# Statistics of two rows on ScalarE, other orders at two norm boundaries, copies ahead of preparation, and last columns apart

## What is computed

```python
def first_block(x, c, ...):
    x = layer_norm(x, emb_ln_g, emb_ln_b)
    sh1, sc1, gt1, sh2, sc2, gt2 = split(silu(c) @ w_ada + b_ada, 6)
    p = (x * (1.0 + sc1) + sh1) @ w_in
    mix = concat([gmlp(p[..., :1024]), rwkv7(p[..., 1024:])]) @ w_out
    x = layer_norm(ALPHA * x + gt1 * mix, ln1_g, ln1_b)      # boundary 1
    gu = (x * (1.0 + sc2) + sh2) @ w_ffn_in                  # hidden size 2816
    f = (silu(gu[..., :2816]) * gu[..., 2816:]) @ w_ffn_out
    return layer_norm(ALPHA * x + gt2 * f, ln2_g, ln2_b)     # boundary 2

def second_block(x, ...):
    u = rms_norm(x, norm_mix_pre) @ w_in                     # behind boundary 2
    y = concat([sparse_attention(u), short_conv(u)]) @ w_out
    x = x + rms_norm(y, norm_mix_post)
    gu = causal_dwconv(rms_norm(x, norm_ffn_pre) @ w_ffn_up, ffn_conv_w)
    y = (gelu(g) * up) @ w_ffn_down                          # g, up: halves of gu
    return x + rms_norm(y, norm_ffn_post)
```

## Time and profile before

| | |
|---|---|
| Median of 3 runs | 1444.79 us (1439.49 to 1449.67) |
| Profiled execution | 1449.72 us |
| Its span, first to last instruction | 1447.9 us |
| Mean granted TensorE clock | 0.982 |
| Instructions | 23058 |
| HBM traffic | 146.5 MB |

### The profile page before, as it was taken

The page is one execution under the profiler, slowest core; times in us unless marked ns, Lnnn a source line. Parts: engine busy times, 40 slices in busy tenths (PEclk is TensorE's granted clock), DMA queues, the critical chain, the costliest instruction groups (busy, mean ns, idle before and its releaser), DMA issues.

```text
span 1447.9 us, 23058 instructions
## 1 busy us (share of the span) xinstructions
PE 1380.8 (95%) x9570; PEld 1140.0 (79%) x9570; DVE 697.5 (48%) x1197; ACT 562.3 (39%) x846; POOL 468.9 (32%) x132
## 2 busy tenths in 40 slices
PE   5999999899999999999998999999999999999998
PEld 3788766776888888888887678888788888888886
DVE  6645586463664433453336525687355445443002
ACT  4444554252343223222124434555355343343122
POOL 0223243024324434434520231112213344344344
PEclk9999999998999999999999989999999999999999
DMA  8763166002222232233213520101221322322311
GB/s 334 241 137 114 59 239 229 3 4 87 88 88 88 87 117 88 87 116 116 88 61 124 202 88 4 56 30 59 74 88 59 117 87 88 116 88 102 116 58 58
DMA packets 24741, 147.93 MB, mean 102 GB/s; under 512 B 2716, under 2 KB 3868, under 8 KB 9024
## 3 DMA queue, kind: packets, MB, share of 16 engines
q1 hardware_dynamic: 21128, 134.21, 25.4%
q10 hardware_dynamic: 3512, 12.26, 3.3%
HBM read 141.74 MB, written 4.72 MB: 101 GB/s over the span
## 4 chain that ended last, share of the span: by engine, by line
PE 84%; DVE 7%; ACT 3%; issue 2%; POOL 2%; DMA 2%; SPq 0%; DVEq 0%; ACTq 0%; POOLq 0%
PE bank L2073 23%; PE bank L2075 22%; PE bank L2074 22%; PE bank L2377 5%; PE bank L1169 2%; POOL weight_lo L1302 2%; DMA raw<-in_weights 2%; PE bank L1160 1%; PE bank L1151 1%; PE bank L2256 1%; ACT weight_hi L1350 1%; PE bank L2190 1%; PE bank L2237 1%; PE bank L1078 1%; DVE xres L1685 1%
## 5 line engine op out<-in xcount | busy, mean ns | idle before, releaser
L1302 POOL TENSOR_TENSOR weight_lo<-raw,weight_hi 128x2048 fp32r<-128x2048 f32 (+2 forms) x91 | 418.4, 4598 | 834.8 <-ACT weight_hi L1350 834.7
L2073 PE MATMUL bank<-act_hi,weight_hi 128*128 128x512 f32 (+1 forms) x1136 | 434.1, 382 | 10.0 <-POOL weight_lo L1302 3.7
L2075 PE MATMUL bank<-act_hi,weight_lo 128*128 128x512 f32 (+1 forms) x1136 | 424.6, 374 | 0.0
L2074 PE MATMUL bank<-act_lo,weight_hi 128*128 128x512 f32 (+1 forms) x1136 | 424.6, 374 | 0.0
L1350 ACT ACTIVATE weight_hi<-raw 128x2048 fp32r<-128x2048 f32 (+1 forms) x98 | 185.2, 1891 | 398.3 <-PE bank L2075 397.5
L2073 PEld LDWEIGHTS bank<-act_hi,weight_hi 128*128 128x128 f32 x1136 | 215.6, 190 | 52.1 <-issue 8.6
L2075 PEld LDWEIGHTS bank<-act_hi,weight_lo 128*128 128x128 f32 x1136 | 215.3, 190 | 38.5
L2074 PEld LDWEIGHTS bank<-act_lo,weight_hi 128*128 128x128 f32 x1136 | 215.6, 190 | 34.5
L2074 PE MATMUL bank<-weight_lo,hid_hi 128*128 128x512 f32 x352 | 136.9, 389 | 0.0
L2073 PE MATMUL bank<-weight_hi,hid_hi 128*128 128x512 f32 x352 | 136.9, 389 | 0.0
L2075 PE MATMUL bank<-weight_hi,hid_lo 128*128 128x512 f32 x352 | 136.9, 389 | 0.0
(11 more groups left out here) (370 smaller groups left out, 1760.1 us busy)
## 6 DMA issues: line engine op xcount, KB each, us to landing
raw<-in_weights SPq DMA_DIRECT2D x120, 1024.0 KB, 4.6
w<-in_w ACTq DMA_DIRECT2D x2, 2048.0 KB, 11.9
bias_rows<-grow ACTq DMA_DIRECT2D x1, 2560.0 KB
xres<-in_x SPq DMA_DIRECT2D x4, 512.0 KB, 6.2
strip<-bias_rows ACTq DMA_DIRECT2D x1, 2048.0 KB, 9.5
out<-xres SPq DMA_DIRECT2D x3, 512.0 KB, 2.6
row_a<-in_ln_g ACTq DMA_DIRECT2D x2, 512.0 KB, 4.1
row_b<-in_ln_b ACTq DMA_DIRECT2D x2, 512.0 KB, 4.9
```

Of the source, the lines that this page charges most:

```text
L1302: pool.tensor_tensor(wlo[i % SPLIT][:, :size], raw[n % RAW][:, :size], whi[i % SPLIT][:, :size], ALU.subtract).then_inc(lo_ready, 1)
L2073: pe.matmul(o, l[0], r[0], start=first, stop=False)
L2074: pe.matmul(o, l[0], r[1], start=False, stop=False)
L2075: return pe.matmul(o, l[1], r[0], start=False, stop=last)
```

## The change

- **Who makes low parts.** VectorE no longer makes that of slc, and makes those of up1_2 (behind boundary 1) and up2_2 (behind boundary 3); GpSimd makes slc's.
- **Input projection.** The steps of `ACT_EARLY` run in the next unit's turn of the loop, behind its `convert()` and ahead of its drains.
- **Boundary 1.** The turn of the first half stands ahead of the last tile's products of the last out1 unit. ScalarE normalises a half's first row as soon as its root is there, ahead of the copy of up1_0 in the first half, and ahead of the root of the second row. VectorE takes the reciprocal of the first row between the gating and the sums of the second row (first half), or ahead of them (second half).
- **Boundary 2.** Statistics of tiles 1 and 3 are taken by ScalarE (`rows_stats`: one pass with an accumulator for the mean, one of squared differences, the root); VectorE only writes the sum (`scaled_rows`), and its first normalising pass of tiles 1 and 3 reads `xres`, for tile 3 in place. So the banks of tile 3 are drained by `scaled_rows`, ahead of tile 2's normalisation. The copy of slc stands ahead of `affine_half`.
- **The end.** In `squares_of_rows` the first sum is scaled between the two squares. The last tile of the last ff2 unit is multiplied by column halves: both k of the first bank, then both of the second.

```diff
@@ -133,7 +133,7 @@
 RAW, SPLIT = 3, 2
-BY_VECTOR = [UNIT_AT[name] for name in ("lora0", "k0", "out1_3", f"down1_{FT // 2 - 1}", "slc", "out2_3", "up2_1")]
+BY_VECTOR = [UNIT_AT[name] for name in ("lora0", "k0", "out1_3", f"down1_{FT // 2 - 1}", "out2_3", "up2_1", "up1_2", "up2_2")]
@@ build
...
+    S = {n: sem(n) for n in ("summed", "gated", "row2_ready", ...
...
@@ -800,12 +800,12 @@
-            for j in range(2):
+            first, second = squares[:, 2 * t:2 * t + 1], squares[:, 2 * t + 1:2 * t + 2]
+            for j, total in enumerate((first, second)):
                 await_full(act, (stage, t, j))
-                a.step(act.activation(temp[:, 0:SEQ], bank((stage, t, j))[:], ACT.Square,
-                                      accum_out=squares[:, 2 * t + j:2 * t + j + 1]), drain((stage, t, j), "act"))
-            first, second = squares[:, 2 * t:2 * t + 1], squares[:, 2 * t + 1:2 * t + 2]
-            a.step(act.activation(first, first, ACT.Identity, bias=eps[:, 1:2], scale=1.0 / DM))
+                a.step(act.activation(temp[:, 0:SEQ], bank((stage, t, j))[:], ACT.Square, accum_out=total), drain((stage, t, j), "act"))
+                if j == 0:
+                    a.step(act.activation(first, first, ACT.Identity, bias=eps[:, 1:2], scale=1.0 / DM))
             a.done(act.activation(rstd[:, t:t + 1], second, ACT.Sqrt, bias=first, scale=1.0 / DM), S["rms_root"])
@@ -1045,8 +1045,7 @@
             affine_lo_half("h4", half, "nfp")
-            if half == 0:
-                low_part("up2_1")
+            low_part(f"up2_{1 + half}")
         for m in range(FT):
@@ -1450,9 +1449,11 @@
-        for name in W_IN1:
+        for name, previous in zip(W_IN1, ("", *W_IN1)):
             if name not in ("lora1", "k1", W_IN1[-1]):
                 convert()
+            for step in ACT_EARLY.get(previous, ()):
+                prep_act(*step)
             if name in ("lora0", "lora1"):
@@ -1469,15 +1470,11 @@
                     bias_rows()
-                for step in ACT_EARLY.get(name, ()):
-                    prep_act(*step)
             elif name[:2] == "pu":
...
                            drain((name, j), "act"))
-                for step in ACT_EARLY.get(name, ()):
-                    prep_act(*step)
                 if name == "pu1":
@@ -1610,10 +1605,10 @@
             root_of_variance(2 * half, TT + 2 * half)
+            normalise_row(2 * half)
             if half == 0:
...
             root_of_variance(2 * half + 1, TT + 2 * half + 1)
-            normalise_row(2 * half)
             normalise_row(2 * half + 1)
@@ -1638,12 +1633,24 @@
-            if (e, t) == (0, 2):
-                act.wait_ge(S["row2_ready"], 2)
+            if e == 0 and t >= 2:
+                act.wait_ge(S["row2_ready"], 2 * (t - 1))
             else:
...
+        def rows_stats(t):
+
+            if t == 1:
+                act.wait_ge(S["summed"], 2)
+            else:
+                for j in range(2):
+                    await_drained(act, ("ff1", t, j), "dve")
+            mean, var = mv[:, t, 0:1], mv[:, t, 1:2]
+            a.step(act.activation(xn2[:, t, :], xres[:, t, :], ACT.Identity, scale=1.0 / DM, accum_out=mean))
+            a.step(act.activation(xn2[:, t, :], xres[:, t, :], ACT.Square, bias=mean, scale=-1.0, accum_out=var))
+            a.done(act.activation(rstd[:, t:t + 1], var, ACT.Sqrt, bias=eps[:, 0:1], scale=1.0 / DM), S["root1"])
+
         def root_x(e, t):
@@ -1655,17 +1662,17 @@
             t, u = 2 * half, 2 * half + 1
-            root_of_variance(t, 2 * TT + t)
+            root_of_variance(t, 2 * TT + half)
+            rows_stats(u)
             if half == 0:
                 convert()
-            root_of_variance(u, 2 * TT + u)
             for x in (t, u):
...
                 scaled_x(0, x)
-            affine_half("h3", half, "nmp")
             if half == 0:
                 convert()
+            affine_half("h3", half, "nmp")
         second_act(act, a, convert, affine_half, square_x, root_x, scaled_x)
@@ -1956,13 +1963,15 @@
-        def residual(stage, t, gate, keep=False):
+        def residual(stage, t, gate, keep=False, between=()):
...
                     tt(bank((stage, t, j))[:], bank((stage, t, j))[:], gate[:, h], ALU.mult)
+            for x in between:
+                inverse(1 + x, x)
             for j, h in enumerate(halves):
@@ -1971,6 +1980,13 @@
             d.step(V.bn_aggr(mv[:, t, :], stats[:]), S["var1"])
+
+        def scaled_rows(t, sem=None):
+
+            for j in range(2):
+                name, h = ("ff1", t, j), slice(SEQ * j, SEQ * j + SEQ)
+                await_full(dve, name)
+                stt(xres[:, t, h], xres[:, t, h], ALPHA, bank(name)[:], ALU.mult, ALU.add, sem=sem or drain(name, "dve"))
@@ -2002,12 +2018,15 @@
                 residual("mix1", t, acc[:, 0:DM])
-            residual("mix1", u, acc[:, 0:DM])
-            for x in (t, u):
-                inverse(1 + x, x)
+            if half:
+                inverse(1 + t, t)
+            residual("mix1", u, acc[:, 0:DM], between=() if half else (t,))
+            inverse(1 + u, u)
             if half == 0:
...
             affine_lo_half("h2", half, 2)
+        low_part("up1_2")
+
         def gated_unit(n):
@@ -2035,10 +2054,10 @@
             halves = [slice(SEQ * j, SEQ * j + SEQ) for j in range(2)]
-            kept = t != 2
+            kept = t < 2
             of = [bank(("ff1", t, j))[:] if kept else xres[:, t, h] for j, h in enumerate(halves)]
             for j, h in enumerate(halves):
-                stt(of[j], of[j], mv[:, t, 0:1], row2_a[:, h], ALU.subtract, ALU.mult)
+                stt(of[j], of[j] if t == 0 else xres[:, t, h], mv[:, t, 0:1], row2_a[:, h], ALU.subtract, ALU.mult)
             for x in between:
@@ -2050,17 +2069,15 @@
             if half == 0:
-                residual("ff1", u, None, keep=True)
+                scaled_rows(u, S["summed"])
+            else:
+                scaled_rows(u)
             second_norm(t)
-            if half:
-                residual("ff1", u, None, keep=True)
             second_norm(u, between=(t,))
...
             affine_lo_half("h3", half, "nmp")
-            if half == 0:
-                low_part("slc")
         second_dve(dve, d, ts, tt, stt, affine_lo_half, inverse_x, low_part)
@@ -2122,10 +2139,10 @@
-        def rows_product(stage, n, n_units, weights, parts, t, k, turned=False):
+        def rows_product(stage, n, n_units, weights, parts, t, k, turned=False, banks_of=range(2)):
             (hi, lo), (hi_in, lo_in) = weights, parts
-            for j in range(2):
+            for j in banks_of:
                 c, f = slice(SEQ * j, SEQ * j + SEQ), 2 * ((n + 2) % 4 if turned else n) + k
@@ -2148,7 +2165,7 @@
                 if n == n_units - 1:
-                    order = [(t, k) for t in range(TT) for k in range(2)]
+                    order = [(t, k) for t in range(TT - 1) for k in range(2)]
                 if ready is not None and n in ready:
@@ -2159,6 +2176,9 @@
             if not halves:
+                for j in range(2):
+                    for k in range(2):
+                        rows_product(stage, n_units - 1, n_units, weights, parts, TT - 1, k, turned, (j,))
                 return
@@ -2195,7 +2215,7 @@
             for half in range(2):
-                if (half, stage) not in ((1, "h2"), (0, "h4")):
+                if (half, stage) not in ((1, "h2"), (0, "h2"), (0, "h4")):
                     turn_half(stage, half, source, ready)
@@ -2594,7 +2614,8 @@
-        dense_rows("mix1", "out1", 4, (act_hi, act_lo), begun, {2: (S["y_lo"], 2), 3: (S["y_lo_last"], 2)})
+        dense_rows("mix1", "out1", 4, (act_hi, act_lo), begun, {2: (S["y_lo"], 2), 3: (S["y_lo_last"], 2)},
+                   turn=("h2", xres, (S["xn_ready"], TT)))
         dense_halves(("up1_0", "up1_1"), "h2", xres, (S["xn_ready"], TT))
```

More of the change, by code:

```diff
@@ L603, in build @@
                                           "bias", "out", "rel", "tabs", "w1", "strip0", "strip", "rows3", "rows4")}
-    S = {n: sem(n) for n in ("gated", "row2_ready", "consts_ready", "silu_c", "future_ready", "xn_ready", "affine1", "h_hi", "h_lo", "shift_ready", "lora_ready",
+    S = {n: sem(n) for n in ("summed", "gated", "row2_ready", "consts_ready", "silu_c", "future_ready", "xn_ready", "affine1", "h_hi", "h_lo", "shift_ready", "lora_ready",
                              "kk_raw", "kk_sq", "cs_ready", "exp_ready", "minus_ready", "r_ready", "ep_ready", "rows_free", "root_ready", "inverse_ready", "norm_root", "prep_ready",
```

## The result

| | before | after |
|---|---|---|
| Median, runs of one occasion | 1444.23 us (1438.23 to 1451.87, 7 runs) | 1428.95 us (1428.15 to 1432.88, 7 runs) |
| Ratio | | 0.9883, 95% interval 0.9861 to 0.9906 |
| Profiled execution | 1449.72 us | 1430.69 us |
| Its span | 1447.9 us | 1428.9 us |
| Mean granted clock | 0.982 | 0.989 |

The account below looks back on a forecast made before the run. TensorE, busy 1380.8 of 1447.9 us, was taken to bound the kernel. Terms of 3.4 + 3.4 + 6.4 + 0.8 + 0.4 = 14.4 us off the median 1444.79 gave 1430.4 us, range 1422 to 1440.

Parts of the forecast that it names:

- Input projection: At v1, pv1 and pu0: TensorE's waits for GpSimd's low parts go, 3.4 us gained, bounds 0 and 3.5.
- Boundary 1: mix1 to up1: VectorE's and ScalarE's rows come sooner, up1_2's wait goes; 3.4 us gained, bounds 1.6 and 4.
- Boundary 2: ff1 to cmp, slc: less work on VectorE, shorter wait, last turn at full clock; 6.4 us gained, bounds 4.4 and 7.
- chain of collisions: Input projection: GpSimd's earlier low parts block VectorE near 103, 126 and 140 to 145; slack at pu1 at least 1.4 us.
- projection eaten: Rival at the input projection: collisions hold VectorE longer, pu1's low part becomes the new wait; gain 11, 1434 us; chance 0.15.
- Collision: Rival at boundary 2: tile 1's normalising pass overlaps GpSimd's cmp, TensorE starts 3.9 us later; gain 10.5, 1434.3 us; chance 0.12.
- up2_2 and the end: up2_2's low part on VectorE gains 0.8 us; at the end, earlier squares and scaling gain 0.4 us.
- bank claim: At up2_2: TensorE claims a bank drained after two operations of up2_0's convolution; 0.2 us given back.
- clock helps more: Rival: fewer waits spare half-clock stretches elsewhere, 2 to 8 us more; 1425 us; chance 0.11.
- within 1%: Whole kernel: change too small to tell from none, chance 0.56, against 0.40 faster and 0.04 slower; bound at 1430.3 us.

Follow-up runs that it names:

- e9: The changed kernel with the first turn of boundary 1 behind the last products again, all else as changed; one run, 1433.6 us.
- e3: The kernel before with only boundary 2 changed; 1434.53 us (4 runs), ratio 0.9910.
- e6: The changed kernel once more, unchanged, with a second profile; 1429.68 us (6 runs), ratio 0.9880.
- e11: The changed kernel with boundary 2 as before; 1437.18 us (6 runs), ratio 0.9935.
- e12: The kernel before with only boundary 2 changed, same kernel as e3 on another occasion; 1438.80 us (10 runs), ratio 0.9944.
- e7: The changed kernel with slc's low part back on VectorE; 1431.84 us (4 runs), ratio 0.9896.
- e10: The kernel before with 36 idle matmuls in TensorE's wait ahead of boundary 2's second turn; 1443.40 us (10 runs), ratio 0.9989.
- e8: The changed kernel with slc's high copy behind the activation copies, as before; 1427.97 us (4 runs), ratio 0.9872.
- e5: The kernel before once more, unchanged, with a second profile; 1447.68 us (12 runs), ratio 1.0000.

## Why the prediction was right

**Bound and method.** TensorE's starts decide; each term was read as "who ends last here". All five places came out within 0.4 us of their terms (boundary 2 in the first pair 6.8 for 6.4, the others 0.1), and the sum 0.5 above, 14.9 for 14.4 (14.6 with boundary 2's 6.4 of the other traces).

- **Input projection, forecast 3.4.** 3.5 measured, no wait at the three units. The chain of collisions went as forecast (103, 126, and 139 instead of 140 to 145), and pu1's low part came at 157.8, within 157.1 to 158.4. So "projection eaten" did not happen. One detail was missed: which operation the lock hits at 126.
- **Boundary 1, 3.4.** 3.5. With all borders moved by 3.55 us, the last turn starts 1.84 sooner (402.84 for 404.68, forecast 2.1). The last product of up1_1 starts 2.2 sooner (419.23 for 421.44), so some 0.4 goes with the clock of turn and products (forecast 0.3); 1.1 more is gained at up1_2 (forecast 0.99) and 0.1 behind it. e9 gives the early turn its 0.6; the two other changes of order weren't run apart.
- **Boundary 2, 6.4.** 6.4 in e3, e6, e11 and e12; 6.8 against the first trace, whose slow stretch was the longer. On the clock of before, moved by 7.02, VectorE's last row ends at 777.5 (forecast 777.9), the last diagonal at 779.7 (780.15), the wait is 0.55 (0.3). Half 0 gave 0.7 where 0.3 was forecast. Parts: slc 2.2 (e7; 2.29), clock 1.4 to 1.8 (e10; 1.9); the rest is put down to statistics and root, which no run took by themselves.
- **Collision.** Forecast at 755.0 to 756.6 against GpSimd's start at 757.0; measured 747.98 to 749.54 against 749.99, that is 755.00 to 756.56 against 757.01 on the clock of before. It missed by 0.45 us, where the forecast had 0.4. e8 shows what it would have cost.
- **up2_2 and the end, 0.8 and 0.4.** 0.86 and 0.32, with 0.23 left ahead of up2_2 (forecast 0.2). The profile names no releaser for it; VectorE's second convolution operation there ends at about 1084.3 (four from 1082.71 in 3.10 us), just ahead of TensorE's 1084.34, as the forecast's bank claim has it.
- **Clock elsewhere.** The profiled execution took 1430.69 us where 1435.3 was forecast, and 4.4 of this are in attention. Its stretch at half clock was 17.1 us in before and 6.8 in the changed kernel, but also 6.8 in the unchanged e5, and 17.1 again in the changed e7 and e9. Row of e7:

```profile
842.70:859.80 17.10, 16.19 (x55) 13.93 (x55) 7.51 (x27) 3.71 (x13) 3.46 (x1) 0.50 0.18 62
```

So this differs from execution to execution, with the change and without it. Whether the long stretch has become rarer isn't shown: it stands in five of the seven traces with the old boundary 2 and in two of the seven with the new.

**The 1%.** The chances leaned to "within 1%" (0.56), and the result is 1.2%, its interval 0.94% to 1.39%. What the sum lacked is gain beyond its five places: the medians of the first occasion are 15.3 us apart for the 14.4 of the sum. Over the 70 runs the mean of before is 1446.8, e6's is 1429.5: 17.3 us. The base doesn't explain this, since 14.4 off 1446.8 is 1.0% too. But it made the time look better than the sum was: 1444.79, the median of three runs of a kernel whose runs differ by 14 us, lay 2.0 under the long mean, and that hid most of the 2.9 that the gain lacked. That the time came out 1.5 us off is in this part luck.

The mark of the clock fell by 8.7 us (22.3 to 13.6). The stretches at half clock that went at the boundaries (3.4 to 6.8 between 387 and 408, 3.4 to 6.8 between 775 and 788, over the traces of kernels with the old order there) make 3.4 to 6.8 of it; what is left are fewer or shorter stretches elsewhere.

**What stays open.** The places give 14.6 to 14.9, the medians of the first occasion 15.3, the means 17.3. The timed kernels gained 1 to 2 us more than their places show (e11 9.4 for 8.1, e12 8.1 for 6.4), within their intervals of some 3.5 us either way. Whether fewer waits also make the half clock a little rarer elsewhere, as the rival "clock helps more" had it, isn't settled; by e12 it isn't the large effect that e3 suggested. The 0.4 us of the recurrence are open too. Not run apart were the statistics on ScalarE and, at the end, the scaling between the squares and the order by column halves.

## What to carry to other kernels

A chain of hand-ordered work can be forecast to some tenths of a us if each place is walked instruction by instruction, down to which operation starts inside another engine's. Before a new wait is put down to a change, look for it in a second trace of the kernel without the change. Where runs of one kernel differ by 1% through the clock, judge a change of half a per cent by its segments in the traces, and take ten or more timed runs before a ratio is believed.

## What the runs showed of the hardware

- A copy of 128 x 8 numbers on VectorE took 4.20 us for 0.17, because it began 0.45 us after a GpSimd subtraction over SBUF tensors; the copy has one input only. Its end (130.30) is GpSimd's end (130.28). VectorE's operations with one input in a bank went on beside GpSimd at their usual 0.7 us (e8, two in 1.41 at 755.64).
- ScalarE's statistics of a row of 1024 cost 1.06 us for the sum, 1.15 for the squared differences, and 0.19 for each read of the accumulator, 2.4 us from the first start to the last end (744.42 to 746.84), where VectorE's two bn_stats and one aggregate cost 1.6. It pays since ScalarE was idle there.
- The granted clock, averaged over an execution, went from 0.979 to 0.992 over the 70 runs of the kernel before, and 0.001 of it is 1.45 us of the mark used above.
